# Two-block transformer forward pass: the branch on further expert rounds turned round, table entries behind the first rows, closing expert pair of 64 and 64

## What is computed

```python
x = rmsnorm(h)                                   # 512 x 1024
group = argmax(x @ w_group + b_group)            # one group of experts per token
e1, e2 = top2(x @ w_expert + b_expert in group)  # two experts per token
for e in experts:                                # 32 of hidden 256 in block 1, 16 of hidden 512 in block 2
    y += weight[:, e] * ((silu(x @ w_gate[e]) * (x @ w_up[e])) @ w_down[e])
```

## Time and profile before

| | |
|---|---|
| median of 3 runs | 1435.55 us |
| the profiled execution, its time | 1433.75 us |
| its span in the profile | 1432.0 us |
| PE busy | 1309.0 us (91%) |
| DVE, ACT, POOL busy | 35%, 26%, 21% |
| mean granted TensorE clock | 0.973 |
| read from memory, written | 258.62 MB, 29.06 MB |

### The profile page before, as it was taken

One profiled execution on the slowest core, in us unless ns is written; L12 is line 12 of the kernel. 1 busy time (PEld: TensorE's weight loads), 2 busy tenths in 40 slices (PEclk: granted clock), 3 DMA queues, 4 the chain that ended last, 5 costly groups with the idle time before them and its releaser, 6 DMA issues. The chain is left out here.

```text
span 1432.0 us, 26492 instructions
## 1 busy us (share of the span) xinstructions
PE 1309.0 (91%) x11524; PEld 851.9 (59%) x11524; DVE 504.9 (35%) x935; ACT 366.3 (26%) x680; POOL 307.8 (21%) x350
## 2 busy tenths in 40 slices
PE   7999989888899999998969999998899899989994
PEld 6778754577645654454448878896545554444432
DVE  6278335432334321111173157653522501001016
ACT  2323147344222111111142242233522211111112
POOL 8354212254000200000023422450000211111100
PEclk9999999999999999999989999999999899999997
DMA  6812000300073799999951111103052589999983
GB/s 222 300 59 82 37 1 0 120 4 4 4 269 118 281 416 416 416 417 418 412 192 60 59 60 59 60 1 118 1 188 94 208 344 357 412 411 416 404 349 145
DMA packets 75339, 284.03 MB, mean 198 GB/s; under 512 B 14966, under 2 KB 16317, under 8 KB 62930
## 3 DMA queue, kind: packets, MB, share of 16 engines
q1 hardware_dynamic: 68592, 267.47, 47.8%
q0 software_dynamic: 5056, 10.56, 2.0%
q10 hardware_dynamic: 1570, 4.24, 0.8%
HBM read 258.62 MB, written 29.06 MB: 201 GB/s over the span
## 5 line engine op out<-in xcount | busy, mean ns | idle before, releaser
L390 POOL TENSOR_TENSOR arena_mix<-ring 128x512 f32<-128x512 f32 x52 | 69.3, 1351 | 170.6 <-PE banks L425 124.8
L1705 PE MATMUL banks<-ring,mixT 128*128 128x512 f32 x224 | 99.1, 595 | 3.9 <-PEq L50 3.2
L435 ACT ACTIVATE arena_mix<-banks 128x256 f32<-128x256 f32 x104 | 39.4, 382 | 234.5 <-PE banks L425 234.5
L2059 POOL DMA_INDIRECT expert_rows<-arena_moe x21 | 20.5, 974 | 366.1 <-ACT arena_moe L2386 183.8
L425 PE MATMUL banks<-ring 128*128 128x256 f32 x416 | 96.2, 380 | 1.6 <-DVE arena_mix L446 1.0
L2101 DVE TENSOR_TENSOR mixT<-banks,params 128x512 f32<-128x512 f32 (+2 forms) x64 | 38.1, 596 | 140.5 <-PE banks L2076 83.2
L446 DVE SCALAR_TENSOR_TENSOR arena_mix<-banks,arena_mix 128x256 f32<-128x256 f32 x78 | 32.0, 422 | 156.8 <-ACT arena_mix L435 89.0
L425 PEld LDWEIGHTS banks<-ring 128*128 128x128 f32 x416 | 78.3, 190 | 14.0 <-issue 3.6
L2076 PE MATMUL banks<-G_moe,x_hi_moe 128*128 128x256 f32 (+2 forms) x320 | 82.0, 295 | 4.5 <-issue 4.5
L2076 PE MATMUL banks<-G_moe,x_lo_moe 128*128 128x256 f32 (+2 forms) x320 | 80.3, 290 | 0.0
L425 PE MATMUL banks<-ring,arena_mix 128*128 128x256 f32 x320 | 72.4, 380 | 0.7 <-ACT arena_mix L435 0.7
(11 more groups left out here) (511 smaller groups left out, 2554.0 us busy)
## 6 DMA issues: line engine op xcount, KB each, us to landing
ring<-in_w_in SPq DMA_DIRECT2D x26, 1024.0 KB, 7.5
arena_moe<-in_exp_w_gate SPq DMA_DIRECT2D x16, 1024.0 KB, 12.4
arena_moe<-in_exp_w_up SPq DMA_DIRECT2D x16, 1024.0 KB, 16.4
arena_moe<-in_exp_w_down SPq DMA_DIRECT2D x16, 1024.0 KB, 16.0
ring<-in_exp_w_gate SPq DMA_DIRECT2D x16, 1024.0 KB, 12.8
ring<-in_exp_w_up SPq DMA_DIRECT2D x16, 1024.0 KB, 15.5
ring<-in_exp_w_down SPq DMA_DIRECT2D x16, 1024.0 KB, 17.6
arena_moe<-in_w_gate SPq DMA_DIRECT2D x8, 2048.0 KB
```

The lines of the kernel that those rows point to most:

```text
L390: pool.tensor_tensor(out[:, c], a[:, c], b[:, c], op).then_inc(ph.sem("weight_sums"), 1)
L435: act.activation(self.dest(n, i)[block], self.m.banks[a][:, 0:256], ACT.Copy, scale=self.scale(n)).then_inc(ph.sem(name), 1)
L1705: last = pe.matmul(m.banks[k % 3][:], m.mixT[:, c, i * P:(i + 1) * P], w[:, c, :], start=(c == 0), stop=(c == DC - 1), skip_group_check=True)
L2059: pool.indirect_dma_start(z.d.outputs, bass.IndirectOffsetOnAxis(ap=place[:, c:c + 1].bitcast(U32), axis=0), z.y[:, 2 * c:2 * c + 2, :].re ...
```

## The change

It has three parts.

1. PE and DVE branch on "no further rounds" instead of on "further rounds". The first rows and, on PE, all of body 0 stand inside the way that is taken, directly behind the comparison; the further rounds and a second copy of the first rows (and body 0) stand in the other way, behind it. The other engines branch as before.
2. On DVE `entries` is taken out of the stretch ahead of the branch and put behind the four copies of the first rows. Only the split stays ahead (`last_split`).
3. In block 2 the last pair has 64 slots for either expert. The experts' order puts the two with fewest tokens there, the condition for further rounds is more than six over 64, the table of slots is loaded with 10 DMAs and not 8, body 6 transposes 128 rows and not 160, and the last body, its sums and its read-back are written anew. The read-back waits for the first gate/up of the last body, not for the second.

```diff
-        self.main_loads = 128 if self.wide else 32
+        self.main_loads = 160 if self.wide else 32
...
-        return self.slots if body == 0 or not self.wide else self.cap + 64
+        if body == 0 or not self.wide:
+            return self.slots
+        return P if body == self.bodies - 1 else self.cap + 64
...
-    part(0, 0, 0, E, 0, 0, z.cap)
-    part(z.cap, 0, 0, E - 1, 1, 32, 32)
+    part(0, 0, 0, E - 2, 0, 0, z.cap)
+    part(z.cap, 0, 0, E - 2, 1, 32, 32)
+    part(0, 0, E - 2, E - 1, 0, 0, 64)
+    part(64, 0, E - 2, E - 1, 1, 0, 64)
...
+    def last_split(dve):
+
+        split(dve, NT - 1)
+
     def entries(dve):
 
-        split(dve, NT - 1)
...
-    v.link(dve.scalar_tensor_tensor(many, many, 7.0, z.stat[:, 2, 0:1], ALU.is_gt, ALU.max))
+    v.link(dve.scalar_tensor_tensor(many, many, float(z.bodies - 2), z.stat[:, 2, 0:1], ALU.is_gt, ALU.max))
...
+    def run_ahead(self, engine, begin, body, end, ahead, none, behind):
+
+        n = self.rounds_of(engine)
+        with engine.If(n < 1):
+            none()
+        with engine.Else():
+            ahead()
+            self.repeat(engine, n, begin, body, end, False)
+            behind()
...
+def one_sums_pe(pe, ph, m, z):
+
+    def half(t, n):
         for part in (z.y_hi, z.y_lo):
...
+            last = pe.matmul(m.banks[2 * t + n][:], z.ST[:, 0, t * P:(t + 1) * P], part[:, n, :], start=(part is z.y_hi),
+                             stop=(part is z.y_lo))
+        if n == 1:
+            last.then_inc(ph.sem("summed"), 1)
...
-    sp.wait_ge(ph.sem("hidden"), z.units * (z.bodies - 1) + (2 if z.wide else 1))
+    sp.wait_ge(ph.sem("hidden"), z.units * (z.bodies - 1) + 1)
...
-    further.run(pe, lambda r: None, body, end)
+    further.run_ahead(pe, lambda r: None, body, end, lambda: None, first, first)
...
-    further.run(dve, begin, body, lambda n: dve.nop())
+    def rows_and_entries():
+        first()
+        entries(dve)
+
+    further.run_ahead(dve, begin, body, lambda n: dve.nop(), lambda: entries(dve), rows_and_entries, first)
...
+        def last_gate_up(u):
...
+                for half in range(2):
+                    last = pe.matmul(hb[u][64 * half:64 * half + 64, :], z.xe[:, j, 64 * u:64 * u + 64],
+                                     both[:, :, j, half * 256:half * 256 + 256], start=(j == 0), stop=(j == DC - 1),
+                                     skip_group_check=True)
+            last.then_inc(ph.sem("hidden"), 1)
...
+        def last_body():
+            last_gate_up(0)
+            last_gate_up(1)
+            turn_hidden(ph, NB - 1, 0)
+            turn_hidden(ph, NB - 1, 1)
+            pe.wait_ge(ph.sem("y_taken"), 3 * (NB - 1))
+            last_down()
...
-        body(0)
-        for i in range(1, NB):
+        def first_body():
+            first_rows_pe(pe, ph, out, z, gath, yb[0:2])
+            body(0)
+
+        further_pe(pe, further, z, x, x_ring, extra_body, first_body)
+        for i in range(1, NB - 1):
             packed_body(i)
-        all_sums_pe(pe, ph, m, z, 2, 3)
+        last_body()
+        one_sums_pe(pe, ph, m, z)
...
         early(0)
+        y_low_dve(dve, ph, z, 0, yb[0], z.main.weight[:, NB - 1, 0:1])
         early(1)
-        rest_hidden(NB - 1)
+        y_low_dve(dve, ph, z, 1, yb[1], z.main.weight[:, NB - 1, 0:1])
         early(2)
         early(3)
-        for i in range(3):
-            y_low_dve(dve, ph, z, i, yb[i], z.main.weight[:, NB - 1, i // 2:i // 2 + 1], HW if i < 2 else 256)
...
+        for u in range(2):
+            silu(ph, NB - 1, u)
+        act.preload_act_table_set(SQRT)
+        hidden_taken(ph, NB - 1, 0)
+        hidden_taken(ph, NB - 1, 1)
```

More of the change, by code:

```diff
@@ L1631, in load_slots @@
         if self.wide:
-            part(0, 0, 0, 32, self.cap)
+            for first, last, rank in ((0, self.E - 2, 32), (self.E - 2, self.E - 1, 0)):
+                src = table[bass.ds(first_rank + rank, self.cap), first:last, :]
+                engine.dma_start(slots.rows[0:self.cap, 0, first:last, :], src).then_inc(sem, 16)
             part(self.cap, 0, 1, 64, self.cap - 64)
@@ L1958, in order_experts @@
     E = z.E
-    first = z.bodies
+    first = z.bodies - 1
     v.link(dve.scalar_tensor_tensor(z.keys, z.totals, float(E), z.tie, ALU.mult, ALU.add))
@@ L2167, in all_sums_pe @@
     pe.wait_ge(ph.sem("y_low"), both)
-    if z.wide:
-        quarter_sums_pe(pe, ph, m, z, 0)
-        for t in range(2, NT):
-            sums_pe(pe, ph, m, z, t, 0, False)
-        quarter_sums_pe(pe, ph, m, z, 2)
-        return
     for t in range(2):
@@ L2331, in body, with vector @@
             down(ph, i, 1, ring_sems)
-        further_pe(pe, further, z, x, x_ring, extra_body)
-        first_rows_pe(pe, ph, out, z, gath, yb[0:2])
-        for i in range(NB):
+        def first_body():
+            first_rows_pe(pe, ph, out, z, gath, yb[0:2])
+            body(0)
+        further_pe(pe, further, z, x, x_ring, extra_body, first_body)
+        for i in range(1, NB):
             body(i)
         all_sums_pe(pe, ph, m, z, 2, 4)
-    def vector(dve, early):
+    def vector(dve, early, entries):
         def hidden(ph, g, u):
@@ L2451, in first_rows_pe, with further_pe @@
     gather_pe(pe, ph, z, second, 1, None)
-def further_pe(pe, further, z, x, x_ring, body):
+def further_pe(pe, further, z, x, x_ring, body, first):
     def end(n):
@@ L2463, in end, with further_dve @@
         pe.sem_inc(x.sem("reloaded"), 1)
-    further.run(pe, lambda r: None, body, end)
-def further_dve(dve, further, z, x, rest):
+    further.run_ahead(pe, lambda r: None, body, end, lambda: None, first, first)
+def further_dve(dve, further, z, x, rest, entries, first):
     def begin(r):
@@ L2736, in next_rows, with last_down @@
             else:
-                turn_rows_pe(pe, ph, m, z, gath, half, 32 * (n - 1), taken, z.width(n))
+                turn_rows_pe(pe, ph, m, z, gath, half, 32 * (n - 1) - (16 if n == NB - 1 else 0), taken, z.width(n))
+        def last_gate_up(u):
+            pe.wait_ge(ring[u], 32 * NB)
+            both, _ = z.expert(u)
+            for j in range(DC):
+                if u == 0 and j % 2 == 0:
+                    pe.wait_ge(ph.sem("gathered_taken"), 4 * (NB - 1) + j // 2 + 1)
+                for half in range(2):
[3 more added lines that the diff above has]
+            last.then_inc(ph.sem("hidden"), 1)
+        def last_down():
+            pe.wait_ge(ph.sem("turned_hidden_taken"), 3 * (NB - 1) + 2)
+            for s in range(2):
+                pe.wait_ge(ring[2 + s], 16 * NB)
+            for n in range(2):
+                for h in range(2):
+                    for f in range(2):
+                        for s in range(2):
+                            _, wd = z.expert(s)
+                            last = pe.matmul(yb[n][64 * s:64 * s + 64, :], z.hT[:, s, f, 64 * h:64 * h + 64],
+                                             wd[:, 2 * h + f, n * HW:(n + 1) * HW], start=(h == 0 and f == 0),
+                                             stop=(h == 1 and f == 1), skip_group_check=True)
+                last.then_inc(ph.sem("down"), 1)
+        def last_body():
[5 more added lines that the diff above has]
+            last_down()
         def packed_body(i):
@@ L2884, in scalar @@
             leave(2)
+        for u in range(2):
[3 more added lines that the diff above has]
+        hidden_taken(ph, NB - 1, 1)
+        for n in range(2):
+            act.wait_ge(ph.sem("down"), 3 * (NB - 1) + n + 1)
+            y_high_act(act, ph, z, n, yb[n], z.main.weight[:, NB - 1, 0:1])
     return sync, gpsimd, tensor, vector, scalar
```

113 lines of the change are left out of this document (56 added, 57 removed).

## The result

The changed kernel is slower. Its median is 1446.48 us (13 runs, 1443.44 to 1454.31) against 1435.93 us of the kernel before (13 runs, 1429.99 to 1445.14); the ratio of all these runs is 1.0068, with a 95% interval of 1.0047 to 1.0090. The forecast was 1430.8 us, and the range ended at 1438. The profiled execution took 1443.44 us, its span is 1441.7 us against 1432.0, so 9.7 us have to be found.

The account below looks back on a forecast made before the run. Both blocks' experts were taken as bound by the weight stream, except block 2's first three bodies, bound by PE. Terms 3.0 + 0.4 + 0 - 8.2 = -4.8 us took the profiled 1433.75 to 1429.0, median 1430.8 us; range 1426 to 1438.

Parts of the forecast that it names:

- The branch on PE: Block 2's gather starts 3.5 us earlier, worth nothing as body 1 waits for weights; nothing to gain in block 1.
- Entries in block 2: SP waits for the slot table, so body 1's first weights go out 10.3 us later; net +3.0 us, bounds 0 and 10.3.
- 7.3 come back: Block 2's 36.6 MB up to 1245 us take 87.7 us at 417 GB/s instead of 95, returning 7.3 us.
- the sign that the prediction named: In block 2, the window from 1160 to 1245 us would move over 400 GB/s if the forecast was right.
- Rival A: The late slot table counts in full in both blocks: +4.7 us in sum, 1440.3 us; chance 0.12.
- Entries in block 1: The late two experts' weights are issued 2.6 us later, mostly covered: +0.4 us, bounds 0 and 2.6.
- cover: Block 1: 4.2 MB of loads issued from 484.59 keep DMA busy 10.1 us and some start-up, to about 496.
- The jump behind body 0: PE's jump over the other way, priced 3.5 us in each block; taken as 0, or 7.0 us if nothing covered it.
- rival B: The stall returns uncovered behind body 0 of both blocks: +2.2 us in sum, 1437.8 us; chance 0.08.
- The closing pair: End of block 2: final additions start at 1407.3 instead of 1415.48, -8.2 us, bounds -4 and -10.
- Rival C: The tail gives half, DVE still waiting for the read-back: -4 instead of -8.2, 1435.0 us; chance 0.15.

Follow-up runs that it names:

- The jump made short: Changed kernel with entries back ahead of DVE's branch, PE's branch turned and PE's other way left empty: 1422.42 us, ratio 0.9915 to the kernel before.
- the closing pair alone: Only part 3 of the change put on the kernel before, both branches and the entries as before: 1419.75 us against 1429.36, ratio 0.9928.
- the repeat: Second measurement, on another chip, of the changed kernel with PE's branch as before and entries behind the first rows: 1440.78 us, ratio 1.0022.

## Why the prediction was wrong

**The branch on PE: right.** The gather starts behind the router's last matmul without idle time, 3.4 us earlier against the rest of block 2 (1130.12 - 1124.84 = 5.3 later, and block 2 begins 8.7 later), and what it is worth is an earlier table: the first weights go out 40.9 us behind the block's first count and not 44.2. The prediction had counted that in its 10.3. The jump made short, which has that gain alone, is 0.9915 against the pair's 0.9928: not to be told apart.

**Entries in block 2: the delay right, its price wrong.** "The first weights of body 1 are issued at 1158.4, 10.3 us later" was 10.2 us. The step that failed is "7.3 come back". It took the 385 GB/s up to 1245 for slack that a late stream could fill at block 1's 417. With the entries behind and PE's branch as before that stream did run full, at 400 GB/s and a share of 0.99, nearly the sign that the prediction named, and took 228.0 us, 6.2 less than in the kernel before. But the closing pair alone takes 228.4 us with its weights on time: the same time was counted as the delay's rebate that the pair has anyway. So the delay is charged almost in full, 10.9 us (272.2 - 261.3) and not 3.0. In the changed kernel the long jump lengthens the stream again, to 233.3 us, with 363 GB/s in its first stretch and a DMA share of 0.82 from 1196.5 to 1204: SP issues a load only when PE has read its buffer, so a stopped PE leaves a gap in the stream. Rival A had the late table in full, at 0.12 only.

**Entries in block 1: mis-sized.** Forecast +0.4 (0 to 2.6), measured 5.1 us (657.4 - 652.3), and 6.0 in the repeat. I took the 12.1 us from entries to table from block 2. In block 1 it was 18.0 us (entries end at 481.36, table at 499.34). The waits of SP's queue in the changed kernel say for what:

```profile
SPq L1631 <- DMA slot_table<-arena_moe: 11.7, 1, 11.7
```

It is the landing of the scatters, of which the last was issued at 491.78, among the weight loads of the same body. The late two experts' weights went out 9.1 us later (8.2 against the block's start) and not 2.6. The window of before for the same stretch,

```profile
488.00:500.00 12.00, 12.00 (x74) 6.84 (x71) 1.80 (x3) 1.15 (x4) 1.19 (x6) 1.00 1.02 421
```

has 421 GB/s where the changed kernel's has 330: the 4.2 MB that I had named as cover ran out.

**The jump behind body 0: the other step that failed.** "I take 0; if nothing covered it, 7.0 us." Measured alone it costs 659.4 - 652.3 = 7.1 us in block 1 and 267.1 - 261.3 = 5.8 in block 2. Two errors: it was priced like the jump of 94 matmuls, though it passes over 248 and 436 and comes in two pieces; and "weights are late anyway" is no cover: the jump makes the stream 5.3 us longer where it is late (233.3 against 228.0 us) and 6.5 where it isn't (234.9 against 228.4). I had written that by the rule of the Trainium skill (Runtime: NRT & Kernel Launch, "Instruction fetch mechanics") the stall is only moved, and comes in block 1 too; rival B, which had that at 0.08, was right in its mechanism, and its 7.0 us for both blocks were about half of the 12.9 measured.

**The closing pair: right.** Forecast -8.2; the tail is 8.4 us shorter in the changed kernel and 7.4 to 9.4 in the others except one, the repeat with the entries behind (5.8). On one chip the pair alone gives 9.6 us. 3.5 us of the profiles' difference lie in block 2 ahead of the tail (264.8 against 261.3). The shorter idle ahead of the gather (2.76 for 4.49) is no part of it, as the gather starts 7.6 us behind the first count and before 7.4. PE reaches body 1 1.8 us sooner, by first strips of 14.0 us for 16.5; the rest I can't place. The read-back was later than I thought: it waits for the scatter of body 6, 9.03 us in the chain of waits, and DVE's first addition waited until 1413.24. It cost some 0.3 us: the second low part, which stands behind it in DVE's queue, could not start before ACT's high part ended at 1419.41, and started at 1419.72. Rival C had that wait, but thought it worth half the gain.

**The sum.** Forecast +3.0 + 0.4 + 0 - 8.2 = -4.8. Measured in the spans +7.8 (block 1) + 9.4 (block 2) - 8.4 (tail) + 0.9 (ahead) = +9.7. Taken singly the errors would be larger (7.1 + 5.8 for the jump, 5.1 + 10.9 for the entries), but together they cost 9.3 in block 1 and 12.9 in block 2 over the pair alone. In block 2 most of the difference of 3.8 us is the 3.3 us by which the turned branch makes the table less late. Rivals A and B were given as alternatives, each against the rest as forecast; that both could hold at once wasn't priced, and the range of 1426 to 1438 fell short for that.

**Left open.** Why PE is slow in the first strips of block 2. It falls in the time in which POOL scatters the entries, in a stretch of the shortest matmuls. With the entries behind it took 7.4 to 8.2 us more in four of five profiles, with the entries ahead 0 to 3.6 us. In the changed kernel no packet of instructions comes in it, so it isn't the stall of the jump. No run took the scatters away, so their part isn't shown, nor why one profile was free of it.

## What to carry to other kernels

Turning a branch round doesn't remove a jump, it moves it to the end of the way that is taken, and whatever is copied into the other way makes it longer: put the short and rare code there, and count how many instructions the jump passes over before you price it.
Work that sits ahead of weights in an issuing queue is part of the critical path when the stream behind it runs full from there on. A share of 0.96 in the kernel before is no promise that a late stream gets time back: compare the length of the stream, from its first issue to its last landing, with and without the delay (228.4 and 228.0 us here). When two delays hit the same bodies, test each alone, since either can hide the other; here it showed that each undid the gain. Here the version to keep is the closing pair alone, 0.9928 of the kernel before.

## What was new about the hardware

- A jump on PE over 68 or 94 matmuls behind a long body was free in one profile with the DMA engines at a share of 1.01, though the same 94 cost 3.4 us ahead of the gather. Over 132 and 158 it cost 1.90 and 3.25 us, over 248 and 436 two pieces of up to 3.8 and 5.2 us, the second after 1 to 16 more records.
- PE's stalls behind jumps can be read off the DMA queue "q8 instruction": all 19 end 1.2 to 1.7 us behind the landing of a 16 KB packet, while the jump over nothing has none.
- Behind the stall of 8.2 us PE's granted clock was 0.62 over 4.4 us, so for most of it at its lower level (1.2 and not 2.4 GHz).
- POOL's eight small scatters of entries took 1.3 us from start to start in both blocks of the changed kernel, but from the start of the last to SP's first table load it was 7.6 us with weights in the queues (491.78 to 499.34) and 2.1 us without (1157.20 to 1159.33).
